# Two transformer blocks on one core: first transfers spread over two queues, first row scaled on ScalarE, later stores and three small orders changed

## The reference, cut

```python
def first_block(x, c, ...):
    mod = jax.nn.silu(c) @ ada_w + ada_b                      # 6 x 1024 numbers
    shift1, scale1, gate1, shift2, scale2, gate2 = split(mod, 6)
    u = rms_norm(h, norm1_g) * (1 + scale1) + shift1          # "the first row"
    z = u @ w_in
    ...                                                       # q, k, v of NSA and stick-breaking, gates
    h = h + gate1 * mixed
    ff = jnp.square(relu(u2 @ mlp_w1)) @ mlp_w2
    return h + gate2 * ff

def second_block(x, mem, ...):
    x = x + 0.5 * swiglu(rmsnorm(x, ffn1_norm), ffn1_w_gu, ffn1_w_down)
    ...                                                       # spatial gating, MLA, memory attention
    x = x + merged @ w_out                                    # "mix2"
    x = x + 0.5 * swiglu(rmsnorm(x, ffn2_norm), ffn2_w_gu, ffn2_w_down)
    return x
```

## Time and profile before

| | |
|---|---|
| median of 3 runs | 1038.56 us (1038.42 to 1039.31) |
| the profiled execution | 1034.66 us |
| its span (first to last instruction) | 1032.9 us |
| PE busy | 1025.3 us, 99% |
| DVE, ACT, POOL busy | 808.3, 614.8, 47.3 us |
| DMA, mean over the span | 202 GB/s |
| DMA, first 52 us (two slices of 40) | 355 and 411 GB/s |

### The profile page before, as it was taken

The page is one execution under the profiler, slowest core; times in us unless marked ns, Lnnn a source line. Parts: engine busy times, 40 slices in busy tenths (PEclk is TensorE's granted clock), DMA queues, the critical chain, the costliest instruction groups (busy, mean ns, idle before and its releaser), DMA issues.

```text
span 1032.9 us, 18991 instructions
## 1 busy us (share of the span) xinstructions
PE 1025.3 (99%) x6926; PEld 933.1 (90%) x6926; DVE 808.3 (78%) x1486; ACT 614.8 (60%) x1140; POOL 47.3 (5%) x74
## 2 busy tenths in 40 slices
PE   8999999999999999999999999999999999999998
PEld 7999998999988888888888899899999998888887
DVE  7998988988988555598887867666877869888753
ACT  5497688547665444565654557796554466555532
POOL 1011100020100000000000100000000010000000
PEclk9999999999999999999999999999999999999999
DMA  9998855776866666666666655555445546666663
GB/s 355 411 359 286 275 174 165 234 260 218 307 186 186 191 191 185 183 187 190 191 187 187 190 175 164 154 153 164 123 123 153 174 149 200 189 192 189 185 191 113
DMA packets 58366, 208.94 MB, mean 202 GB/s; under 512 B 7041, under 2 KB 8449, under 8 KB 57771
## 3 DMA queue, kind: packets, MB, share of 16 engines
q1 hardware_dynamic: 52474, 184.72, 58.2%
q0 software_dynamic: 5808, 23.09, 6.4%
HBM read 204.62 MB, written 3.16 MB: 201 GB/s over the span
## 4 chain that ended last, share of the span: by engine, by line
PE 92%; DVE 6%; issue 2%; ACT 1%; DVEq 0%; ACTq 0%
PE bank L682 90%; DVE ring_rounded L1873 2%; PE bank L1043 1%; DVE ada_ring L1929 1%; DVE body L1929 0%; DVE u L1969 0%; DVE u_rounded L1975 0%; ACT body L1573 0%; DVE body L1989 0%; ACT rounded_rounded L1413 0%; DVE body L2163 0%; ACT body L1505 0%; DVE body L2167 0%; DVE part L2163 0%; DVE body L2118 0%
## 5 line engine op out<-in xcount | busy, mean ns | idle before, releaser
L682 PE MATMUL bank<-u_rounded,rounded_rounded 128*128 128x256 f32 (+1 forms) x2152 | 506.8, 328 | 1.4 <-issue 1.0
L1873 DVE TENSOR_TENSOR ring_rounded<-ring,rounded_rounded 128x1024 fp32r<-128x1024 f32 x326 | 397.2, 1224 | 114.1 <-ACT rounded_rounded L1413 103.2
L1413 ACT ACTIVATE rounded_rounded<-ring 128x1024 fp32r<-128x1024 f32 x326 | 342.8, 1054 | 111.5 <-PE bank L682 100.6
L682 PE MATMUL bank<-u_rounded,ring_rounded 128*128 128x256 f32 x1504 | 350.3, 281 | 0.0
L682 PEld LDWEIGHTS bank<-u_rounded,rounded_rounded 128*128 128x128 f32 x2152 | 332.7, 188 | 4.9 <-issue 2.0
L682 PE MATMUL bank<-body_rounded,rounded_rounded 128*128 128x256 f32 (+1 forms) x1296 | 321.1, 335 | 0.2 <-DVE body L2163 0.2
L682 PEld LDWEIGHTS bank<-u_rounded,ring_rounded 128*128 128x128 f32 x1504 | 282.8, 188 | 37.1
L682 PE MATMUL bank<-body_rounded,ring_rounded 128*128 128x256 f32 x952 | 217.0, 280 | 0.0
L682 PEld LDWEIGHTS bank<-body_rounded,ring_rounded 128*128 128x128 f32 x952 | 178.9, 188 | 26.4
L682 PEld LDWEIGHTS bank<-body_rounded,rounded_rounded 128*128 128x128 f32 x1296 | 201.1, 188 | 1.4 <-issue 0.4
L1668 ACT ACTIVATE part<-bank 128x256 f32<-128x256 f32 x65 | 24.9, 383 | 78.5 <-PE bank L682 78.5
(11 more groups left out here) (276 smaller groups left out, 892.2 us busy)
## 6 DMA issues: line engine op xcount, KB each, us to landing
ring<-in_stream SPq DMA_DIRECT2D x328, 512.0 KB, 3.7
ada_ring<-in_ada POOLq DMA_DIRECT2D x32, 512.0 KB, 5.4
body<-in_ada SPq DMA_DIRECT2D x8, 512.0 KB, 9.2
ada_ring<-in_ada SPq DMA_DIRECT2D x6, 512.0 KB, 8.3
mem_parts_kept<-body_rounded POOLq DMA_DIRECT2D x2, 1024.0 KB, 7.3
body_rounded<-mem_parts_kept POOLq DMA_DIRECT2D x2, 1024.0 KB, 5.2
x<-in_x_t SPq DMA_DIRECT2D x2, 512.0 KB, 4.7
body<-in_mem_t SPq DMA_DIRECT2D x2, 512.0 KB, 7.0
```

The source lines that it names most:

```text
L682: return nc.tensor.matmul(out, lhs, rhs, start=start, stop=stop, skip_group_check=True)
L1413: a(R(slot_round(q)), slot_weights(n), ACT.Copy).then_inc(slot_rounded, 1)
L1873: v.tensor_tensor(R(w), w, R(slot_round(q)), ALU.subtract).then_inc(slot_split, 1)
```

## The change

Eight edits in one:

1. ACT issues the second half of x and cols at its start, ahead of its table load; SP issues buckets and table behind the first two ring slots.
2. tanh, silu and the spread of c go in halves, and DVE copies c out before it waits for cols.
3. The first row: DVE makes x * row_rinv between the two sums of a k; ACT makes the scale (128x1) and from both u and, unrounded, u_lo; DVE's low part is a plain subtraction.
4. DVE splits slot 16 before it adds the squares of mem up.
5. The matrices are reordered; the last four and the positions are loaded later, by POOL, with waits where they are first used.
6. The high parts of mem are stored in two halves and the low parts later, each with a semaphore of its own, in another order on POOL; `sbw` and a buffer of `nsa_weights` move, and ACT waits for the halves at the two gate blocks ma0 and ma4 instead of for everything before the first stick-breaking step.
7. At the end of mix2, DVE adds blocks 6 and 7 before low parts 4 and 5.
8. Block f2d7 of the last swiglu uses `project` and one residual add.

The diff, cut:

```diff
@@ sp @@
             sp.dma_start(c_line, c_d).then_inc(loaded["c"], 16)
-            for half, name in ((slice(0, 4), "x"), (slice(4, 8), "x_end")):
-                sp.dma_start(x[:, half, :], x_t[:, half, :]).then_inc(loaded[name], 16)
-            sp.dma_start(cols[:, :], cols_d).then_inc(loaded["cols"], 16)
+            sp.dma_start(x[:, 0:4, :], x_t[:, 0:4, :]).then_inc(loaded["x"], 16)
             for k in range(RING // 2):
                 load_ada_early(k)
+                for r in (2 * k, 2 * k + 1):
+                    load(r, r)
                 if k == 0:
                     sp.dma_start(buckets, buckets_d).then_inc(loaded["bias_in"], 16)
                     sp.dma_start(table[:, :], table_d).then_inc(loaded["bias_in"], 16)
-                for r in (2 * k, 2 * k + 1):
-                    load(r, r)
...
-            sp.dma_start(mats[:, 1:, :], mats_d[:, 1:, :]).then_inc(loaded["mats"], 16)
+            sp.dma_start(mats[:, 1:LATE_MATRICES, :], mats_d[:, 1:LATE_MATRICES, :]).then_inc(loaded["mats"], 16)
...
@@ pe @@
             def spread_c():
-                pe.wait_ge(c_silu_ready, 1)
-                for h in range(2):
-                    done(mm(claim(f"c{h}")[:, 0:512], mat("ones")[0:1, :], c_line[:, h * 512:(h + 1) * 512], True, True), f"c{h}")
+                for n, h in enumerate(c_halves):
+                    pe.wait_ge(c_silu_ready, n + 1)
+                    done(mm(claim(f"c{n}")[:, 0:512], mat("ones")[0:1, :], c_line[:, h], True, True), f"c{n}")
...
-                    project_wide(f"{p}d{m}", KF2, hidden_parts, (lambda i: pe.wait_ge(hidden_ready, before + i + 1)) if m == 0 else None)
+                    (project if row == ROW_4 and m == KD - 1 else project_wide)(
+                        f"{p}d{m}", KF2, hidden_parts, (lambda i: pe.wait_ge(hidden_ready, before + i + 1)) if m == 0 else None)
...
@@ pool @@
             load_ada(0, ADA_RING)
+            load_ada(ADA_RING, ADA_RING + ADA_IN_KEYS)
+            pool.wait_ge(u_rounded, ROW_MEM * KD + KD // 2)
+            pool.dma_start(mem_parts_kept[0, :, 0:4, :], R(mem_n[:, 0:4, :])).then_inc(mem_hi_stored, 16)
+            evacuated(pool, "cmp_hid_k")
+            load_ada(ADA_RING + ADA_IN_KEYS, ADA_RING + ADA_BEFORE_SB)
+            evacuated(pool, "sbz0")
+            pool.wait_ge(u_rounded, (ROW_MEM + 1) * KD)
+            pool.dma_start(mem_parts_kept[0, :, 4:8, :], R(mem_n[:, 4:8, :])).then_inc(mem_hi_end_stored, 16)
             pool.wait_ge(bias_stored, 16)
             pool.dma_start(bias, bass.AP(bias_rows.tensor, bias_rows.offset, [[1, P], [512, 8], [1, T]])
                            ).then_inc(loaded["bias"], 16)
-            load_ada(ADA_RING, ADA_RING + ADA_IN_KEYS)
-            pool.wait_ge(u_rounded, (ROW_MEM + 1) * KD)
-            pool.dma_start(mem_parts_kept[0], R(mem_n)).then_inc(mem_stored, 16)
+            load_ada(ADA_RING + ADA_BEFORE_SB, ADA_RING + ADA_BEFORE_SB + 2)
             pool.wait_ge(u_ready, (ROW_MEM + 1) * KD)
-            pool.dma_start(mem_parts_kept[1], R(mem_n_lo)).then_inc(mem_stored, 16)
+            pool.dma_start(mem_parts_kept[1], R(mem_n_lo)).then_inc(mem_lo_stored, 16)
...
-            evacuated(pool, "cmp_hid_k")
-            load_ada(ADA_RING + ADA_IN_KEYS, ADA_NSA)
+            load_ada(ADA_RING + ADA_BEFORE_SB + 2, ADA_NSA)
+            pool.dma_start(mats[:, LATE_MATRICES:, :], mats_d[:, LATE_MATRICES:, :]).then_inc(loaded["late_mats"], 16)
+            pool.dma_start(pos_i[:, :], pos_d).then_inc(loaded["pos"], 16)
...
@@ act @@
+            act.dma_start(x[:, 4:8, :], x_t[:, 4:8, :]).then_inc(loaded["x_end"], 16)
+            act.dma_start(cols[:, :], cols_d).then_inc(loaded["cols"], 16)
             nc.scalar.preload_act_table_set("exp_and_others")
             act.wait_ge(loaded["c"], 16)
-            a(c_tanh, c_line, ACT.Tanh, scale=0.5).then_inc(c_tanh_ready, 1)
+            for h in c_halves:
+                a(c_tanh[:, h], c_line[:, h], ACT.Tanh, scale=0.5).then_inc(c_tanh_ready, 1)
...
             for k in range(KD):
+                scale, shift, gain = mod[:, KD + k:KD + k + 1], mod[:, k:k + 1], col("norm1_g", k)
+                act.wait_ge(ada_summed, 2 * k + 1)
+                a(scale, scale, ACT.Identity, scale=gain, bias=gain).then_inc(scale_ready, 1)
                 ahead(f"u{k}", 1)
-                act.wait_ge(u_normed, ROW_X * KD + k + 1)
+                act.wait_ge(scale_ready, k + 1)
+                act.wait_ge(x_normed, k + 1)
                 act.wait_ge(ada_summed, 2 * k + 2)
-                a(R(u[:, k, :]), u_lo[:, k, :], ACT.Identity, bias=mod[:, k:k + 1]).then_inc(u_rounded, 1)
+                a(R(u[:, k, :]), u_lo[:, k, :], ACT.Identity, scale=scale, bias=shift).then_inc(u_rounded, 1)
+                a(u_lo[:, k, :], u_lo[:, k, :], ACT.Identity, scale=scale, bias=shift).then_inc(u_normed, 1)
                 ahead(f"u{k}", 2)
...
-            act.wait_ge(mem_stored, 32)
             sb_log(0)
             for h in range(8):
...
+                if h % 4 == 0:
+                    act.wait_ge(mem_hi_end_stored if h else mem_hi_stored, 16)
                 copy(gates[:, h, :], f"ma{h}", reach=HALVES if h else HALVES - 1)
...
@@ dve @@
...
-                v.scalar_tensor_tensor(out=R(u_lo[:, i, :]), in0=u_lo[:, i, :], scalar=mod[:, i:i + 1], in1=R(u[:, i, :]),
-                                       op0=ALU.add, op1=ALU.subtract).then_inc(u_ready, 1)
-
-            sum_early(0)
-            scaled(0)
+                dve.wait_ge(u_normed, ROW_X * KD + i + 1)
+                v.tensor_tensor(R(u_lo[:, i, :]), u_lo[:, i, :], R(u[:, i, :]), ALU.subtract).then_inc(u_ready, 1)
+
+            def sum_early_with_x(k):
+                sum_early(2 * k)
+                if k == 0:
+                    dve.wait_ge(row_rinv_ready, ROW_X + 1)
+                normed_x(k)
+                sum_early(2 * k + 1)
+
+            sum_early_with_x(0)
             for k in range(KD):
                 ahead(f"u{k}", 1)
                 low_part_of_u(k)
                 ahead(f"u{k}", 2)
                 if k < KD - 1:
-                    sum_early(k + 1)
-                    scaled(k + 1)
+                    sum_early_with_x(k + 1)
+            ahead("vsw0", 3)
             dve.wait_ge(row_squares_ready, (ROW_MEM + 1) * KD)
...
-            dve.wait_ge(mem_stored, 32)
+            dve.wait_ge(mem_lo_stored, 16)
...
                 ahead(f"{last}6")
+                add_mixed(6)
                 low_part(4)
+                add_mixed(7)
+                evacuated(dve, f"{last}{KD - 1}")
                 low_part(5)
-                add_mixed(6)
                 low_part(6)
                 ahead(f"{last}7")
-                add_mixed(7)
-                evacuated(dve, f"{last}{KD - 1}")
                 low_part(KD - 1)
...
-                    add_both(f"{p}d{m}", m, 0.5)
+                    if row == ROW_4 and m == KD - 1:
+                        add_residual(f"{p}d{m}", m, 0.5, reach=False)
+                    else:
+                        add_both(f"{p}d{m}", m, 0.5)
```

55 lines of the change are left out of this document (29 added, 26 removed).

## The result

The changed kernel takes 1043.66 us in the median (1042.02 to 1044.42), the kernel before 1038.92 in the runs beside it (1036.77 to 1040.25): a ratio of 1.0048, 95% interval 1.0028 to 1.0069, 4.7 us slower. The forecast was 1039.5 within 1037.4 to 1041.4, so the sign was right, the time lies above the range, and the size was too small by a factor of four to five.

What follows compares the result with a forecast made beforehand. PE was taken as the bound, a string of matmuls with hardly a gap. Start +2.4, mix2 -1.1 and tail -0.3 gave +1.0, added to the median 1038.56 for 1039.5 us; range 1037.4 to 1041.4.

Steps and rivals of the forecast that it cites:

- When x lands: Start, landing of x's halves: both could land near 6.5; bounds 0 and +0.4 us for row_rinv, 0 taken in the sum.
- the prediction's bound: Landing of x: halves in flight at once share the DMA engines, land near 6.5, and row sums start about 0.36 later.
- fourth rival: Start: the halves of x share the engines, row_rinv 0.36 later shifts the whole loop; total +1.4, 1039.9; chance 0.15.
- The first row's start: From row_rinv to first projection: second sum waits behind x * row_rinv; projection at about 15.55 against 14.34, +1.2 us.
- Each k: First row's loop: ACT enters the chain, period 5.95 us against 5.757, bounds 5.7 and 6.55; PE 2.0 late at k = 7.
- third rival: First row's loop: ACT bounds it, period 6.1 to 6.4; at 6.25 the total is +3.1, 1041.7; chance 0.2.
- Behind the loop: Slots 16 and 17: DVE waits one rounding longer, hole at 60.55 closes, another opens; 0 to +0.8, taken +0.4 us.
- The store and the bias: Modulation loads on POOL: low half's store queued ahead of part of them could delay DVE; 0 to 1 us, 0 taken.
- Mix2 and tail: Last block of mix2: earlier residual add, -1.1 us; last block of second swiglu: one add fewer, -0.3 us.
- the steps up to the eighth k: First row: start at the first projection plus the longer period make PE 2.0 us late at k = 7.

## Why the prediction was wrong

**When x lands: the wrong end, and another mechanism.** The prediction saw that x could land near 6.5, with 0.36 us to pay, and took 0 in the sum. x landed at 6.8, and at 6.6 when nothing but the queue was changed. But the halves didn't share the engines, as the prediction's bound and its fourth rival have it: they landed at 5.1 and 6.8, 1.65 us apart, where one queue had them 1.54 apart. SP issues c first, so ACT's issue of the second half went out 0.41 us ahead of the first half, and it was served first. So the bound had nearly the right time by luck. The Trainium skill (DMA: Bandwidth & Descriptors, "Issuing engines are not separate DMA queues") states that transfers of different issuing engines run on the same engines and interleave, and that a second issuing engine saves issuing time alone. The second part agrees with the traces, as all of x was there at 6.8, and at 6.9 before; an interleaving of the two halves isn't seen. What the second queue saves is 0.85 us of SP's issue time, and it cost 0.7 us of the row sums' start. The first half issued by ACT, with the second on SP, wasn't tried.

**A cost that no step had.** That delay was priced at 0.36 us. In the trace it made PE idle, the clock fell, and it became 2.38: 0.70 of delay and 1.69 of slower row sums. No step asked what an idle PE does to PE's own speed. In the profiled executions it is the largest single error; the run with the spread over 128 rows, with x nearly as late but no fall of the clock, has 0.44 in its place. That the idle stretch makes the clock fall isn't isolated: the clock fell in the three traces that have it (0.48 to 0.63 us) and not in the two that have the 1-row spread near full speed and no such stretch, but the run meant to fill it decided nothing.

**The first row's start: right.** +1.2 from row_rinv to the first projection was predicted, 1.39 was measured.

**Each k: mechanism right, size short.** ACT came into the chain and its rounding behind u_lo set the period, as described; 6.17 was measured, 5.95 predicted. The mis-sized term is the activation: 0.42 was taken from the row of row_rinv, 0.50 from start to start was measured (0.60 each). The way from DVE's sum to ACT was 0.20, of which 0.08 reads the sum out and 0.12 is the handover, rather than 0.05. Seven periods make 1.5 us of that. The trace of before has an Identity with a bias column of 0.49 to 0.51 on ACT, the nearer row, and the new ones have a second column, the scale:

```profile
18.25 0.51 ACT L1498 ACTIVATE u_rounded<-u,mod 128x256 fp32r<-128x256 f32 x1 [0.87 <-DVE u L1969]
```

The Trainium skill (ScalarE: Activation LUTs, "What ACT_TABLE_LOAD costs") gives about 93 ns for each column operand of an activation; the rows agree, 0.42 with none (row_rinv), 0.51 with one and 0.60 with two. The third rival, slower from a period of 6.1 on, was the case: it had a chance of 0.2 and a price of 1041.7.

**Behind the loop: right.** +0.4 predicted, +0.35 measured, with a hole at 69.76 in place of the one at 60.55.

**The store and the bias: outside its bounds.** 0 was taken out of 0 to 1, and it cost 2.2 in the first trace and 1.5 in the second of the same kernel. The step spoke of the low store only. The load of the bias, also 1 MB, was moved from 54 us into the same stretch and wasn't counted, although it stands in the diff; and "PE does not wait there now" is no slack: two late loads used up DVE's lead, and PE waited for DVE in the heads. The run with the early order gives it back, 2.3 us by the traces and some 1.6 by the runs; it moves the bias load and the stores together, so their shares stay open.

**Mix2 and tail: right.** -1.1 and -0.3 predicted, -1.05 and -0.3 measured.

**The median.** The sum of the steps, had it been right, would still have been 7.4 against 4.7: the profiled execution of before was one of the lower group, and I added a difference of its trace to medians of the other. The gap of 3.9 us between its 1034.66 and the 1038.56 was in the prediction, and it was not asked what it was. In the higher groups, where the medians lie, the clock's part falls away: there the spread lasts past the landing of x, and the transfers alone left the higher runs at 1038.6 to 1039.8, as before. What is wrong in the median is the first row (some 4.4 us in either group of the run with it alone, where the steps up to the eighth k had 2.0) and the store with the bias (some 1.6, where 0 was taken).

**What stays open.** In which executions PE gets full speed early isn't settled; the traces show when it came (spread of 1.98, 2.23 or 3.78 us), not why. No execution of the kernel before out of its higher group was traced, so what separates its groups is taken from the other kernels: the traces from lower groups have the early rise and those from higher groups the late one. That the lower runs with the transfers alone lost their 2 us to the clock rests on their mean clock.
